# First weights from ScalarE's queue, the first tile by halves, another order of the early work, and GpSimd's long table products in two pieces, in a hybrid decoder layer

## The reference

```python
h = rms_norm(x, g_mix[l])
z = h @ w_in[l]
q, k, v, u, gate_a, gate_s = jnp.split(z, SPLIT_POINTS, axis=-1)
a = dilated_attention(q, k, v, g_q[l], g_k[l]).astype(x.dtype)
a_out = a @ w_attn_proj[l]
y = s5_ssm(u, lambda_re[l], lambda_im[l], log_dt[l], b_re[l], b_im[l],
           c_re[l], c_im[l], d_skip[l])
y = jax.nn.gelu(y).astype(x.dtype)
s_out = (y @ w_glu_a[l]) * jax.nn.sigmoid(y @ w_glu_b[l])
mix = jax.nn.sigmoid(gate_a) * a_out + jax.nn.sigmoid(gate_s) * s_out
x = x + mix @ w_out[l]
h2 = rms_norm(x, g_ffn[l])
x = x + (jax.nn.silu(h2 @ w_ffn_gate[l]) * (h2 @ w_ffn_up[l])) @ w_ffn_down[l]
```

## Time and profile before

| | |
|---|---|
| median of 3 runs | 886.42 us (885.99 to 886.95) |
| the profiled execution, its own time | 887.11 us |
| its span | 885.3 us |
| TensorE busy | 869.0 us (98%) |
| VectorE busy | 437.6 us (49%) |
| ScalarE busy | 322.9 us (36%) |
| GpSimd busy | 189.7 us (21%) |
| HBM traffic over the span | 122 GB/s |

### The profile page before, as it was taken

One profiled execution on the slowest core, in us unless ns is written; L12 is line 12 of the kernel. 1 busy time (PEld: TensorE's weight loads), 2 busy tenths in 40 slices (PEclk: granted clock), 3 DMA queues, 4 the chain that ended last, 5 costly groups with the idle time before them and its releaser, 6 DMA issues.

```text
span 885.3 us, 12797 instructions
## 1 busy us (share of the span) xinstructions
PE 869.0 (98%) x4441; PEld 717.4 (81%) x4441; DVE 437.6 (49%) x625; ACT 322.9 (36%) x486; POOL 189.7 (21%) x219
## 2 busy tenths in 40 slices
PE   5999999999999999999999999999999999999998
PEld 4888888888897877877887888888888888888886
DVE  5553375687914444444488554333333334433334
ACT  6312343323235656656433343222222222322221
POOL 4699988850020000001220220000000000000000
PEclk9999999999999999999999999999999999999999
DMA  7429334474355542412544233333333332222222
GB/s 277 143 79 254 97 119 145 151 180 160 119 180 161 167 149 82 143 47 87 148 139 184 89 97 94 95 96 100 100 100 100 96 95 96 96 95 95 95 71 95
DMA packets 85936, 108.78 MB, mean 123 GB/s; under 512 B 10672, under 2 KB 51872, under 8 KB 85776
## 3 DMA queue, kind: packets, MB, share of 16 engines
q1 hardware_dynamic: 80096, 96.34, 34.0%
q10 hardware_dynamic: 4400, 8.42, 3.1%
q0 software_dynamic: 1408, 3.61, 1.9%
HBM read 94.38 MB, written 13.96 MB: 122 GB/s over the span
## 4 chain that ended last, share of the span: by engine, by line
PE 53%; DVE 2%; issue 0%; ACT 0%; DVEq 0%; ACTq 0%
PE ps L1401 27%; PE ps L1431 13%; PE ps L1174 12%; DVE late L1156 1%; DVE late L1076 0%; DVE hT_lo L1082 0%; PE ps L1320 0%; PE ps L1306 0%; DVE w_lo L556 0%; ACT w_hi L550 0%; PE ps L1416 0%; DVE late L1079 0%; PE ps L1411 0%; PE ps L1296 0%; DVE late L1007 0%
## 5 line engine op out<-in xcount | busy, mean ns | idle before, releaser
L556 DVE TENSOR_TENSOR w_lo<-w_raw,w_hi 128x1024 fp32r<-128x1024 f32 x142 | 184.6, 1300 | 336.3 <-ACT w_hi L550 336.2
L550 ACT ACTIVATE w_hi<-w_raw 128x1024 fp32r<-128x1024 f32 x142 | 150.4, 1059 | 398.3 <-PE ps L1174 164.0
L1401 PE MATMUL ps<-h_hi,w_hi 128*128 128x512 f32 x352 | 137.2, 390 | 0.0
L1401 PE MATMUL ps<-h_hi,w_lo 128*128 128x512 f32 x352 | 137.0, 389 | 0.0
L1401 PE MATMUL ps<-h_lo,w_hi 128*128 128x512 f32 x352 | 136.9, 389 | 0.0
L407 POOL TENSOR_TENSOR early<-early 128x16 f32<-128x16 f32 (+8 forms) x141 | 128.2, 909 | 23.1 <-ACT early L573 12.3
L1174 PE MATMUL ps<-w_hi,hT_hi 128*128 128x512 f32 x288 | 113.6, 395 | 10.0 <-DVE w_lo L556 10.0
L1174 PE MATMUL ps<-w_hi,hT_lo 128*128 128x512 f32 x288 | 113.0, 392 | 0.0
L1174 PE MATMUL ps<-w_lo,hT_hi 128*128 128x512 f32 x288 | 113.0, 392 | 0.0
L1174 PE MATMUL ps<-hT_hi,w_hi 128*128 128x512 f32 x224 | 91.4, 408 | 0.0
L1174 PE MATMUL ps<-hT_hi,w_lo 128*128 128x512 f32 x224 | 87.6, 391 | 0.0
(11 more groups left out here) (197 smaller groups left out, 1070.4 us busy)
## 6 DMA issues: line engine op xcount, KB each, us to landing
w_raw<-in_w_in SPq DMA_DIRECT2D x112, 256.0 KB, 3.7
w_raw<-in_w_ffn_gate SPq DMA_DIRECT2D x44, 256.0 KB, 2.8
w_raw<-in_w_ffn_up SPq DMA_DIRECT2D x44, 256.0 KB, 3.0
w_raw<-in_w_ffn_down SPq DMA_DIRECT2D x44, 256.0 KB, 2.7
z_d<-early ACTq DMA_DIRECT2D x6, 1024.0 KB, 5.0
late<-z_d SPq DMA_DIRECT2D x96, 64.0 KB
w_raw<-in_w_out SPq DMA_DIRECT2D x16, 256.0 KB, 2.9
z_d<-early SPq DMA_DIRECT2D x3, 1024.0 KB, 5.2
```

Of the source, the lines that this page charges most:

```text
L550: nc.scalar.activation(w_hi[:, j % WSPL], w_raw[:, j % WRAW], ACT.Copy).then_inc(w_hi_done, 1)
L556: nc.vector.tensor_tensor(w_lo[:, j % WSPL], w_raw[:, j % WRAW], w_hi[:, j % WSPL].bitcast(F32), ALU.subtract).then_inc(w_lo_done, 1)
L1401: ins = T.matmul(ps[:, m], (w_hi, w_lo)[b][:, j % WSPL, at_w:at_w + P], (h2_hi, h2_lo)[a][:, 2 * j + h, :], start=j == 0 and h == 0 and k ...
```

## The change

Six things are changed together.

1. The two halves of weight tiles 0 and 1 are loaded from ScalarE's queue ahead of all else there. SyncE loads x in five pieces (k-tiles 0, 1, 2-3, 4-5, 6-7) and then weight tiles 2 and 3.
2. ScalarE runs a one-column activation on a constant after its loads. Tile 0 is rounded and subtracted by halves, each with a semaphore of its own, and TensorE multiplies it half by half: for each half hi x hi, lo x hi, hi x lo over four banks. Thirteen products of `ones` with itself (fp32, 128 columns) go ahead of it on TensorE.
3. ScalarE rounds tile 2 before the second half of the squares, tile 3 before MAG and M8, and tile 4 (U0) before the sines. On VectorE, `lo` of tile 3 comes before the pole steps, that of U0 before `norm_row`, and that of U1 before the copy of `norm_all`.
4. TensorE sums the squares after step 14 of V0 instead of 13.
5. TensorE spreads the norm after two steps of U instead of before U.
6. The cmul of `aB` and that of `ca` on GpSimd run over eight pairs of groups at a time, so that each of their 12 instructions becomes two of half the size.

```diff
+WARM = 13
+X_PIECES = ((0, 1), (1, 2), (2, 4), (4, 6), (6, 8))
...
-            for j in range(4):
-                sp.dma_start(xt[:, 2 * j:2 * j + 2], t["xt"][:, 2 * j:2 * j + 2]).then_inc(xt_loaded[j], 16)
+            for n, (k, k_end) in enumerate(X_PIECES):
+                sp.dma_start(xt[:, k:k_end], t["xt"][:, k:k_end]).then_inc(xt_loaded[n], 16)
+            for j in range(2, 4):
                 load(W_V0 + j, j, in_cols(6))
...
-            tmp = lambda n: toep_f[:, 0:NPR * n * CH].rearrange("p (q k c) -> p q k c", q=NPR, k=n)
-            cmul(aB[:, 0], aB[:, 1], for_k(apw[:, 0], CL), for_k(apw[:, 1], CL),
-                 for_c(bb[:, 0, 0:NPR], CL), for_c(bb[:, 1, 0:NPR], CL), tmp(CL))
+            tmp = lambda n: toep_f[:, 0:8 * n * CH].rearrange("p (q k c) -> p q k c", q=8, k=n)
+            for q in range(0, NPR, 8):
+                eight = slice(q, q + 8)
+                cmul(aB[:, 0, eight], aB[:, 1, eight], for_k(apw[:, 0], CL)[:, eight], for_k(apw[:, 1], CL)[:, eight],
+                     for_c(bb[:, 0, 0:NPR], CL)[:, eight], for_c(bb[:, 1, 0:NPR], CL)[:, eight], tmp(CL))
...
-            cmul(ca[:, 0], ca[:, 1], for_k(apw[:, 0], CL + 1), for_k(apn, CL + 1),
-                 for_c(ctr[:, 0], CL + 1), for_c(ctr[:, 1], CL + 1), tmp(CL + 1))
+            for q in range(0, NPR, 8):
+                eight = slice(q, q + 8)
+                cmul(ca[:, 0, eight], ca[:, 1, eight], for_k(apw[:, 0], CL + 1)[:, eight], for_k(apn, CL + 1)[:, eight],
+                     for_c(ctr[:, 0], CL + 1)[:, eight], for_c(ctr[:, 1], CL + 1)[:, eight], tmp(CL + 1))
...
+            for j in range(2):
+                for h in range(2):
+                    act.dma_start(w_raw[:, j, h * 512:(h + 1) * 512], in_cols(6)(j, h)
+                                  ).then_inc(raw_landed[j] if j or h else raw_first, 16)
+            act.wait_ge(pool_tab, 1)
+            nc.scalar.activation(zsq[:, 0:1], minus_half[:, 0:1], ACT.Copy)
             act.wait_ge(gains_in, 16)
-            for j in range(4):
-                act.wait_ge(xt_loaded[j], 16)
-                for k in (2 * j, 2 * j + 1):
-                    nc.scalar.activation(hT_hi[:, k], xt[:, k], ACT.Copy, scale=gmixT[:, k:k + 1]).then_inc(hT_hi_done, 1)
-                if j < 2:
-                    hi(W_V0 + j, j)
-                if j % 2:
-                    squares(j // 2)
-
-            hi(W_V0 + 2, 2)
+            for h in range(2):
+                act.wait_ge(xt_loaded[h], 16)
+                gained(h)
+                act.wait_ge(raw_landed[0] if h else raw_first, 16)
+                nc.scalar.activation(w_hi[:, 0, h * 512:(h + 1) * 512], w_raw[:, 0, h * 512:(h + 1) * 512], ACT.Copy
+                                     ).then_inc(w_hi_done if h else w_hi_first, 1)
+            for n in range(2, 5):
+                act.wait_ge(xt_loaded[n], 16)
+                for k in range(*X_PIECES[n]):
+                    gained(k)
+                if n != 3:
+                    hi(W_V0 + n // 2, n // 2)
+                if n > 2:
+                    squares(n - 3)
+
             act.wait_ge(params_in, PARAMS)
             nc.scalar.activation(sv[DT], sv[DT], ACT.Exp).then_inc(act_tab, 1)
+            hi(W_V0 + 3, 3)
...
-            hi(W_V0 + 3, 3)
+            hi(W_U, 0)
             act.wait_ge(dve_tab, 10)
...
-            hi(W_U, 0)
...
+            lo(W_V0 + 3, 3)
             dve.wait_ge(act_tab, 1)
             tab(V.tensor_tensor(sv[ANG], sv[LI], sv[DT], ALU.mult))
             tab(V.tensor_tensor(sv[ZR], sv[LR], sv[DT], ALU.mult))
-            lo(W_V0 + 3, 3)
...
+            lo(W_U, 0)
             dve.wait_ge(norm_sums, 1)
             V.tensor_scalar(norm_row[:, :], ps[:, 6, 0:2 * TB].rearrange("p (n e) -> p n e", e=2)[:, :, 0], 1.0 / DM, EPS,
                             ALU.mult, ALU.add).then_inc(norm_eps, 1)
-            lo(W_U, 0)
             dve.wait_ge(norm_done, 1)
             for m in (1, 3):
                 evac_rows(zs[:, 0, m], m, W_V0 + 3)
+            lo(W_U + 1, 1)
             dve.wait_ge(norm_spread, 1)
             V.tensor_copy(norm_all[:, :], ps[:, 7]).then_inc(norm_eps, 1)
...
+            pe.wait_ge(pool_tab, 2)
+            for _ in range(WARM):
+                T.matmul(ps[:, 7, 0:P], ones[:, :], ones[:, :], start=True, stop=True)
+            for h in range(2):
+                for k, (a, b) in enumerate(((0, 0), (1, 0), (0, 1))):
...
+                    for m in range(4):
+                        ins = T.matmul(ps[:, m], h_acts[a][:, h, m * P:(m + 1) * P], (w_hi, w_lo)[b][:, 0, h * 512:(h + 1) * 512],
+                                       start=h == 0 and k == 0, stop=False)
...
-            for _ in range(13):
+            for _ in range(10):
                 next(v0)
             pe.wait_ge(sq_sum, 1)
...
+            u_in = columns(W_U, 4, by_feature, h_acts, sums_read, None, 4)
+            for _ in range(2):
+                next(u_in)
             pe.wait_ge(ident_in, 16)
             pe.wait_ge(norm_done, 1)
```

More of the change, by code:

```diff
@@ L196, in build @@
         params_in = sem("params_in")
-        xt_loaded = [sem(f"xt_loaded{n}") for n in range(TB)]
+        xt_loaded = [sem(f"xt_loaded{n}") for n in range(TB + 1)]
+        raw_first, w_hi_first, w_lo_first = sem("raw_first"), sem("w_hi_first"), sem("w_lo_first")
         gains_in, ident_in = sem("gains_in"), sem("ident_in")
@@ L544, in hi @@
             def hi(w, j):
-                act.wait_ge(raw_landed[j % WRAW], (w - j % WRAW) // WRAW * 32 + 32 if isinstance(w, int)
-                            else 8 * (w - j % WRAW) + 32)
+                landed = 32 if j % WRAW else 16
+                act.wait_ge(raw_landed[j % WRAW], (w - j % WRAW) // WRAW * 32 + landed if isinstance(w, int)
+                            else 8 * (w - j % WRAW) + landed)
                 if not (isinstance(w, int) and w < WSPL):
@@ L794, in _, with gained_lo @@
             dve.wait_ge(gains_in, 16)
-            for j in range(4):
+            def gained_lo(k):
+                dve.wait_ge(hT_hi_done, k + 1)
+                V.scalar_tensor_tensor(out=hT_lo[:, k], in0=xt[:, k], scalar=gmixT[:, k:k + 1],
+                                       in1=hT_hi[:, k].bitcast(F32), op0=ALU.mult, op1=ALU.subtract).then_inc(hT_lo_done, 1)
+            for h in range(2):
+                gained_lo(h)
+                dve.wait_ge(w_hi_done if h else w_hi_first, 1)
+                V.tensor_tensor(w_lo[:, 0, h * 512:(h + 1) * 512], w_raw[:, 0, h * 512:(h + 1) * 512],
+                                w_hi[:, 0, h * 512:(h + 1) * 512].bitcast(F32), ALU.subtract
+                                ).then_inc(w_lo_done if h else w_lo_first, 1)
+            for j in range(1, 4):
                 for k in (2 * j, 2 * j + 1):
[L797 to L800, removed]
+                    gained_lo(k)
                 if j < 3:
                     lo(W_V0 + j, j)
+            lo(W_V0 + 3, 3)
             dve.wait_ge(act_tab, 1)
@@ L828, in _ @@
                 evac_rows(zs[:, 0, m], m, W_V0 + 3)
+            lo(W_U + 1, 1)
             dve.wait_ge(norm_spread, 1)
             V.tensor_copy(norm_all[:, :], ps[:, 7]).then_inc(norm_eps, 1)
-            for j in range(1, 5):
+            for j in range(2, 5):
                 lo(W_U + j, j)
@@ L1206, in gained_rows, with rest_of_first @@
                     pe.wait_ge(hT_lo_done, 2 * j + 2)
-            v0 = columns(W_V0, 4, by_token, h_acts, lambda m: None, gained_rows)
-            for _ in range(13):
+            pe.wait_ge(pool_tab, 2)
+            for _ in range(WARM):
+                T.matmul(ps[:, 7, 0:P], ones[:, :], ones[:, :], start=True, stop=True)
+            for h in range(2):
+                for k, (a, b) in enumerate(((0, 0), (1, 0), (0, 1))):
+                    if k == 0:
+                        pe.wait_ge(hT_hi_done, h + 1)
+                        pe.wait_ge(w_hi_done if h else w_hi_first, 1)
+                    elif k == 1:
+                        pe.wait_ge(hT_lo_done, h + 1)
+                    else:
+                        pe.wait_ge(w_lo_done if h else w_lo_first, 1)
+                    for m in range(4):
+                        ins = T.matmul(ps[:, m], h_acts[a][:, h, m * P:(m + 1) * P], (w_hi, w_lo)[b][:, 0, h * 512:(h + 1) * 512],
+                                       start=h == 0 and k == 0, stop=False)
+                        if h and k == 2:
+                            ins.then_inc(gemm_steps, 1)
+            def rest_of_first():
+                for j in range(1, 4):
+                    yield from products(W_V0 + j, j, False, j == 3, by_token(h_acts, j), None, lambda m: gained_rows(j, m))
+            v0 = rest_of_first()
+            for _ in range(10):
                 next(v0)
@@ L1215, in _, with sums_read @@
             run(v0)
+            def sums_read(m):
+                if m >= 2:
+                    pe.wait_ge(norm_eps, m - 1)
+            u_in = columns(W_U, 4, by_feature, h_acts, sums_read, None, 4)
```

(7 more changed lines are left out.)

2 lines of the change are left out of this document (added).

## The result

The changed kernel takes 888.49 us (median of 20 runs), the kernel before 886.94 us in 20 runs beside it: a ratio of 1.0014, with a 95% interval from 1.0008 to 1.0021. That is slower by 0.08 to 0.21%, the forecast's side and size (a step of 1.1 us from 886.4; the medians stand 1.55 apart, the ratio gives 0.7 to 1.9). One run of 1773.1 us is left out as disturbed. The profiled execution took 889.61 us, the slowest of those left; its span of 887.8 is 2.5 above that of before. A second profile of the same kernel (experiment 5) has 886.5, and is nearer to a usual run. The two are read side by side.

What follows compares the result with a forecast made beforehand. Bound: TensorE's stream and GpSimd's table chain plus 19.2 us of VectorE, meeting at 199.7 us, the tables without slack. Terms -1.9 + 2.4 + 0.9 - 0.3 = +1.1 on 886.4 gave 887.5 us, range 883.5 to 890.2.

Steps and rivals of the forecast that it cites:

- What sets the end: Before the bank at 199.76: GpSimd's tables, k_d stores landing, then 19.2 us of VectorE from `turn_re` without idle time.
- The head, real work near 6.9: TensorE's start: thirteen warm-up products from 1.2 to 6.9 us, then real work, at full pace if the clock rises.
- The table start, -1.9: GpSimd's power ahead of the table products ends at 31.5 instead of 33.4 us, 1.9 earlier (0.6 to 3.1).
- t: Time at which ScalarE can begin on x tiles 2 and 3: 8.9 us, earliest 7.7, latest 10.2.
- The pieces, +2.4: GpSimd's twelve product instructions become 24, at 0.2 us each: 2.4 us later, range 1.2 to 3.6.
- One more collision, +0.9: The VectorE w_lo of 173.74 now falls inside GpSimd's tables: 0.9 us later (0 to 0.9).
- Sum, +1.1 us: Issue of the k_d stores: -1.9 + 2.4 + 0.9 - 0.3, with the eviction before 199.76 moving alike.
- `ca` and bb2 "hold by 0.9": Table results ready at 118.1, before TensorE needs them at 119.0; otherwise its lead is lost here, with the same end.
- TensorE idle for 5 us between 180 and 200, and nowhere else: In the profile after, TensorE's 4.1 us lead becomes 5.2 us of waits behind `turn_re` and at the bank.
- The head reaching the end: Rival: the k_d stores come with TensorE's 4.1 us lead, giving 882.3 us (881.5 to 884.6); chance 0.16.
- The fall of the clock in a pause: Rival: a mid-stream pause of some 3 us halves TensorE's pace, 890.0 us; chance 0.22 together with later tables.
- the third rival: Warm-up doesn't lift the clock, or w_lo 1 is late: TensorE's lead shrinks up to 2.5 us, end unchanged.

Runs made afterwards that it cites:

- experiment 5: The changed kernel run again unaltered, for a second profile; 888.58 us, ratio 1.0013 to the kernel before.
- experiments 3: The kernel before, with turn_re and turn_im using another scratch buffer so VectorE need not wait there for the k_d stores; 887.34 us, ratio 0.9999.
- experiment 4: The changed kernel, with turn_re and turn_im using another scratch buffer so VectorE need not wait there for the k_d stores; 887.64 us, ratio 0.9999.
- Experiment 11: The change with whole products and part 3 (early order on ScalarE and VectorE) undone, except lo of U1; 888.0 us, ratio 1.0010 to the kernel before.
- experiment 6: The change with whole products and another scratch buffer in turn_re and turn_im, without the wait there for the k_d stores; 884.33 us, ratio 0.9967.
- experiment 2: The change without part 6, so the GpSimd products are whole again; 884.15 us, ratio 0.9964 to the kernel before.

## Why the prediction was right, and which of its steps were not

**What sets the end**: right in kind. In all fourteen profiles TensorE's second bank starts 0.80 to 0.81 us after VectorE's eviction begins. In the kernel before and in experiments 3, 4 and 11 TensorE comes to it at nearly the same time (0.31 to 0.32 us from start to start there); in the other ten its lead is lost in pauses of 0.43 to 1.82. The step that failed is the link "land, and VectorE starts `turn_re`", with "from there to the eviction at 198.95 it has no idle time". No idle time, but 1.8 us of held time inside a busy one: the row of L851 in the trace of before (1.95 us for 32 columns, shown under experiment 6) was not read as a wait. The link is the fill of `xst`, 12.06 us after the stores before and 11.22 in the second profile. The stores moved by 2.0 and the eviction by only 1.1, because before GpSimd's loads had to wait 1.1 us for the landing and now start 0.3 behind its own fill.

**The head, real work near 6.9**: 6.64 and 6.78. The warm-up products were over at 5.8 and 6.5 us, not at 6.9; the first real matmul waited for `w_hi` behind them.

**The table start, -1.9**: -2.1 in the second profile (power over at 31.25 against 33.39), -0.2 in the first. For t (8.9, from 7.7 to 10.2) 8.64 was seen in experiment 2, 8.79 in the second profile and 10.29 in the first. How fast x lands varies from run to run, and I know of no cause. Experiment 11's expectation put the gain down to the earlier x pieces alone; with them (8.52) but the order of before the power is over at 35.25. The prediction, which worked the table start out from t and the new order together, was right in this.

**The pieces, +2.4**: 3.1, that is 0.26 each instead of 0.2, inside its range. **One more collision, +0.9**: 0.9 in the products, which the prediction didn't count. The one that it did count came too, in the second profile: that w_lo now begins at 171.75, and a 16-column product beside it takes 1.19 us instead of 0.22. But other collisions behind the products fell away, so that from their end to the stores it is 0.4 more in all. **The stores 0.3 shorter**: no, 2.42 us as before.

**Sum, +1.1 us**: the second profile has -2.3 at the first product, +3.9 over the products, +0.4 between them and the stores, -0.8 at the loads, +1.1 at the bank and 1.2 in the span. That the sum fits so well is partly luck: the missing -0.8 and the underestimated pieces cancel. It fits the second profile and the medians; in the first profile t was just past its late end, the stores were 3.4 later and the bank 2.5.

**`ca` and bb2 "hold by 0.9"**: failed. In the second profile bb2 was ready at 121.12 and TensorE stood from 119.3 on; in the first bb2 came in time (120.83) and the copy L672 did not. The prediction counted w_lo tiles as collisions, and not the small steps of `z_scale` that fall inside the products once these last longer. As it said, the end was the same, the lead was lost sooner. So **"TensorE idle for 5 us between 180 and 200, and nowhere else"** failed: beyond the pace it lost 3.1 us there in the second profile, 2.0 at bb2 and 1.1 at tile 3. **VectorE's wait for k_d of some 10 us** was 5.3 and 7.0.

**The rivals.** The head reaching the end fell: with pieces the end does not move with the head, and without them it moves with the table chain too (-2.4 at the stores, -0.8 at the loads, -3.3 at the bank, where TensorE still pauses). That 884.15 lies in this rival's range of 881.5 to 884.6 is chance. The fall of the clock in a pause was seen three times (the first profile, experiments 4 and 11), at 0.2 us a matmul of 512 columns, and in all three the bank still started 0.8 us behind the eviction's start, so it didn't set the end. The warm-up lifted the clock, so that half of the third rival fell; its other half, w_lo 1 late, came in the first profile (1.87 us), and there too the bank waited for the eviction in the end.

## What to carry to other kernels

Follow the engine that ends a chain down to instructions that last far longer than their size: a step on 32 columns that takes 2 us is a wait, although the trace calls it busy, and the link that it hides may be another than the wait you see. Cutting long GpSimd instructions costs 0.26 us a cut here and helps VectorE only if it can get in between; here, on a chain without slack, they were better left whole. An earlier start pays only as far as each later hand-over (here tile 3, the sums, the power) is moved with it: the order edit carried 3.8 us (the fall of the clock in it), the warm-up at most 0.7, the second queue nothing. The best version found is the change with its products whole, 884.15 us, 0.36% below the kernel before.

## What the runs showed of the hardware that was not expected

A one-input VectorE step of 32 columns in fp32 waited for the whole of a GpSimd fill of 4096 columns (3.54 us), and for the whole of eight fills of 512 issued back to back (3.81 us), while a two-input step of 1024 columns beside such a fill took its usual 1.22 us.

TensorE ran at half pace at once after a pause of 2.3 us shortly after its start (eight matmuls), and five matmuls after one of 3.2 us at 24 us (seven matmuls), both from start to start. In the transposes a pause of 2.24 us of idle time was followed by a granted clock of 0.71 for 5.8 us in experiment 4, one of 2.07 us at the same place in the first profile by a granted clock of 1.00; pauses of 1.7 and 1.8 us from start to start near 190 and 200 us in the second profile left the pace as it was. The half pace at TensorE's first matmuls without a warm-up stands beside a granted clock of 1.00.

The power of four columns on GpSimd took 1.02 us undisturbed and 1.86 to 1.87 against a w_lo.
